# Turning the operands of the last down projection: tokens by channels at the end

## The reference

```python
x = x + rms_norm(groups @ w_out[l], mix_post_norm[l])
h = rms_norm(x, ffn_pre_norm[l])
up = dwconv3(h @ w_up[l], ffn_conv_w[l], ffn_conv_b[l])
gate, val = jnp.split(up, 2, axis=-1)
f = (jax.nn.gelu(gate, approximate=True) * val) @ w_down[l]
x = x + rms_norm(f, ffn_post_norm[l])
```

## Time and profile before

| | |
|---|---|
| median of 3 runs | 1458.9 us |
| profiled execution, its own time | 1459.32 us |
| its span (first to last instruction) | 1457.5 us |
| TensorE matmuls in flight | 1379.8 us, 95% of the span |
| TensorE weight loads | 1029.9 us, 71% |
| VectorE / ScalarE / GpSimd busy | 924.0 / 587.1 / 551.5 us |
| mean granted TensorE clock | 0.989 of full speed |
| the last down projection, first to last matmul start | 1319.05 to 1443.47 us |

### The profile page before, as it was taken

The page is one execution under the profiler, slowest core; times in us unless marked ns, Lnnn a source line. Parts: engine busy times, 40 slices in busy tenths (PEclk is TensorE's granted clock), DMA queues, the critical chain, the costliest instruction groups (busy, mean ns, idle before and its releaser), DMA issues. The chain is left out here.

```text
span 1457.5 us, 15399 instructions
## 1 busy us (share of the span) xinstructions
PE 1379.8 (95%) x5940; PEld 1029.9 (71%) x5940; DVE 924.0 (63%) x992; ACT 587.1 (40%) x864; POOL 551.5 (38%) x287
## 2 busy tenths in 40 slices
PE   7999988988999999999989998988989999999998
PEld 5587654367788888788876785444768888887886
DVE  6776875547778787711186778655478777874113
ACT  5322454534543434432252226444364434343223
POOL 3221332026344444444552215220463434344443
PEclk9999999999999999999999999999999999999999
DMA  7212301012332323233332222100313333323332
GB/s 256 83 29 65 82 13 31 1 57 59 87 101 87 102 87 101 80 101 98 98 131 57 58 54 50 29 15 1 87 58 98 91 99 89 99 85 95 94 93 85
DMA packets 205538, 112.53 MB, mean 77 GB/s; under 512 B 15303, under 2 KB 202425, under 8 KB 204570
## 3 DMA queue, kind: packets, MB, share of 16 engines
q1 hardware_dynamic: 205466, 111.54, 26.3%
HBM read 105.63 MB, written 2.10 MB: 74 GB/s over the span
## 5 line engine op out<-in xcount | busy, mean ns | idle before, releaser
L509 POOL TENSOR_TENSOR wl<-raw,wh 128x1024 fp32r<-128x1024 f32 x176 | 430.2, 2446 | 700.9 <-ACT wh L588 700.9
L588 ACT ACTIVATE wh<-raw 128x1024 fp32r<-128x1024 f32 x176 | 186.5, 1060 | 563.0 <-PE ps L1095 530.4
L1093 PE MATMUL ps<-gh,wh 128*128 128x512 f32 (+1 forms) x864 | 347.5, 402 | 4.8 <-POOL wl L509 4.8
L1095 PE MATMUL ps<-gh,wl 128*128 128x512 f32 (+1 forms) x864 | 342.6, 396 | 0.0
L1094 PE MATMUL ps<-gl,wh 128*128 128x512 f32 (+1 forms) x864 | 342.3, 396 | 0.0
L1093 PEld LDWEIGHTS ps<-gh,wh 128*128 128x128 f32 (+1 forms) x864 | 161.8, 187 | 49.8 <-issue 8.9
L1094 PEld LDWEIGHTS ps<-gl,wh 128*128 128x128 f32 (+1 forms) x864 | 161.8, 187 | 41.9 <-issue 1.9
L1095 PEld LDWEIGHTS ps<-gh,wl 128*128 128x128 f32 (+1 forms) x864 | 161.6, 187 | 40.7
L1533 DVE TENSOR_TENSOR acc<-acc,sq 128x512 f32<-128x512 f32 x24 | 60.6, 2526 | 191.1 <-ACT sq L632 190.8
L1963 DVE SCALAR_TENSOR_TENSOR cv<-pad,pm,cv 128x512 f32<-128x512 f32 x88 | 130.5, 1482 | 78.7 <-ACT cv L952 78.7
L1093 PE MATMUL ps<-fh,wh 128*128 128x512 f32 x308 | 121.7, 395 | 0.6 <-POOL wl L509 0.6
(11 more groups left out here) (274 smaller groups left out, 2211.3 us busy)
## 6 DMA issues: line engine op xcount, KB each, us to landing
raw<-w_up SPq DMA_DIRECT2D x88, 512.0 KB, 3.8
raw<-w_down SPq DMA_DIRECT2D x32, 512.0 KB, 3.8
raw<-w_in SPq DMA_DIRECT2D x30, 512.0 KB, 3.9
raw<-w_out SPq DMA_DIRECT2D x16, 512.0 KB, 4.3
raw<-w_down SPq DMA_DIRECT2D x16, 384.0 KB, 3.3
xio<-x SPq DMA_DIRECT2D x4, 512.0 KB, 4.1
win<-c_win SPq DMA_DIRECT2D x2, 1024.0 KB, 5.6
TF<-c_tf SPq DMA_DIRECT2D x2, 1024.0 KB, 8.9
```

The source lines that it names most:

```text
L509: nc.gpsimd.tensor_tensor(l, raw[:, slot, :], h.bitcast(F32), ALU.subtract).then_inc(S["lo_ready"], 1)
L588: A(xh[:] if third(lay, n) else wh[:, slot, :], raw[:, slot, :], ACT.Copy).then_inc(S["hi_ready"], 1)
L1093: mm(ps[0:cols, bank, :], w_hi, x_hi, start=start and k == 0, stop=False)
L1095: ins = mm(ps[0:cols, bank, :], w_lo, x_hi, start=False, stop=stop and k == tile_n - 1)
```

## The change

In the second layer alone:

- The down projection takes a 128 x 128 block of `fh` or `fl` (128 of its channels by 128 tokens) as stationary operand, and 512 columns of a row block of `w_down` as moving one. All eight PSUM banks hold the sum, bank 2 * tt + dh for token tile tt and half dh of the channels. An item is now one row block of 128 x 1024, so there are 22 instead of 24, the last one (`LAST`) in the third place.
- The order: token tile 0 of blocks 0 and 1, then the rest of these, then blocks 2 to 18 with all eight banks each; then all three last blocks (`TAIL`) bank by bank.
- In the up projection of that layer, after steps 4, 6, ... 18, TensorE transposes four blocks of `xT` into bank 0 or 1, and ScalarE copies the bank to `xres` in the next step.
- The end works on tokens by channels: ScalarE squares a bank with the sum over its columns in the same instruction, and makes the inverse root on one column; VectorE multiplies by the gain (loaded once, on all partitions), then scales and adds to `xres`; SyncE stores each 128 x 512 result. The sum of squares on VectorE, the statistics matmuls, GpSimd's additions, the transposes at the end and their copies go.

The diff, cut to its core:

```diff
-    return n in (2, I_OUT + DC - 1, I_UP + 2, ITEMS - 1)
+    return n in (2, I_OUT + DC - 1, I_UP + 2, ITEMS - 1 if lay < DEPTH - 1 else LAST)
...
+    if lay == DEPTH - 1 and n == LAST:
+        return g - 1
...
+LAST = I_DOWN + FC - 1
+TAIL = 3
...
+        xres = [rope[:, i, :] for i in range(5)] + [w3[:, 0:T], w3[:, T:2 * T], h2[:, 0:T]]
...
+                if lay == DEPTH - 1:
+                    for kk in range(FC):
+                        item(lay, I_DOWN + kk, a["w_down"][lay:lay + 1, kk * P:(kk + 1) * P, :].rearrange("o p (c n) -> o p c n", n=P))
+                    sp.wait_ge(S["f_prod"], DEPTH * FC)
+                    sp.dma_start(cv[:].rearrange("p t n -> p (t n)"), a["ffn_post_norm"][lay, :].partition_broadcast(P)
+                                 ).then_inc(S["g_in"], 16)
+                    continue
...
-            for half in range(2):
-                for c in range(0, DC, 2):
-                    cols, at = slice(c * P, (c + 2) * P), slice(half * TC // 2, (half + 1) * TC // 2)
-                    sp.wait_ge(S["o_copy"], half * DC + c + 2)
-                    sp.dma_start(res[:, at, cols], xout[:, at, cols]).then_inc(S["out_sem"], 16)
+            for tt in range(TC):
+                for dh in range(2):
+                    sp.wait_ge(S["o_done"], 2 * tt + dh + 1)
+                    sp.dma_start(res[:, tt, dh * T:(dh + 1) * T], xres[2 * tt + dh]).then_inc(S["out_sem"], 16)
...
-                for n in range(I_UP + 2, ITEMS + 1 if lay < DEPTH - 1 else ITEMS - 1, 2):
+                for n in range(I_UP + 2, ITEMS + 1 if lay < DEPTH - 1 else LAST, 2):
                     for slot in range(2):
                         lo(lay * ITEMS + n + slot, slot)
-                add(lay, 1)
+                if lay < DEPTH - 1:
+                    add(lay, 1)
...
+                    if lay == DEPTH - 1 and 4 <= j < 20 and j % 2:
+                        g = (j - 4) // 2
+                        act.wait_ge(S["xt_tr"], g + 1)
+                        A(xres[g], ps[:, g % 2, :], ACT.Copy).then_inc(S["xt_copy"], 1)
...
+                if lay == DEPTH - 1:
+                    for n in range(I_DOWN + 3, LAST + 1):
+                        hi(lay, n, n % 2)
+                    continue
...
-            last_square(DEPTH - 1, 1, 0)
-            post(DEPTH - 1, 1, 0)
-            last_square(DEPTH - 1, 1, 1)
-            turned(0, range(2))
-            post(DEPTH - 1, 1, 1)
-            turned(0, range(2, DC))
-            turned(1, range(DC))
+            for tt in range(TC):
+                s0, s1, part, log, r = (st[:, tt, i:i + 1] for i in range(5))
+                act.wait_ge(S["y_done"], 2 * tt + 1)
+                C.do(A(yt[:, 0, :], ps[:, 2 * tt, :], ACT.Square, accum_out=s0))
+                C.join()
+                nc.scalar.sem_inc(S["y_sq"], 1)
+                C.do(A(part, s0, ACT.Identity, bias=eps[:, 0:1], scale=1.0 / DM))
+                act.wait_ge(S["y_done"], 2 * tt + 2)
+                C.do(A(yt[:, 1, :], ps[:, 2 * tt + 1, :], ACT.Square, accum_out=s1))
+                C.join()
+                nc.scalar.sem_inc(S["y_sq"], 1)
+                C.do(A(log, s1, ACT.Ln, bias=part, scale=1.0 / DM))
+                C.join()
+                A(r, log, ACT.Exp, scale=-0.5).then_inc(S["r_inv"], 1)
 
...
+            def turn_stream(g):
+                tt, dh = divmod(g, 2)
+                if g == 0:
+                    pe.wait_ge(S["rbc_ready"], 2 * DEPTH)
+                if g >= 2:
+                    pe.wait_ge(S["xt_copy"], g - 1)
+                for c in range(4):
+                    ins = nc.tensor.transpose(ps[:, g % 2, c * P:(c + 1) * P], xT[:, dh * 4 + c, tt * P:(tt + 1) * P], ident[:])
+                ins.then_inc(S["xt_tr"], 1)
+            def last_down(lay):
+                def part(kk, tt, dh):
+                    h, l = weights(lay, I_DOWN + kk)
+                    bank, rows, cols = 2 * tt + dh, slice(tt * P, (tt + 1) * P), slice(dh * T, (dh + 1) * T)
+                    mm(ps[:, bank, :], fh[:, kk, rows], h[:, cols], start=kk == 0, stop=False)
+                    mm(ps[:, bank, :], fl[:, kk, rows], h[:, cols], start=False, stop=False)
+                    return mm(ps[:, bank, :], fh[:, kk, rows], l[:, cols], start=False, stop=kk == FC - 1)
+                def ready(kk):
+                    item_ready(lay, I_DOWN + kk)
+                    pe.wait_ge(S["f_hi"], lay * FC + kk + 1)
+                    pe.wait_ge(S["f_lo"], lay * FC + kk + 1)
+                pe.wait_ge(S["xt_copy"], DC)
+                for kk in range(2):
+                    ready(kk)
+                    for dh in range(2):
+                        part(kk, 0, dh)
+                pe.wait_ge(S["f_evac"], (lay + 1) * 2 * FC)
+                for kk in range(FC - TAIL):
+                    if kk >= 2:
+                        ready(kk)
+                    for tt in range(1 if kk < 2 else 0, TC):
+                        for dh in range(2):
+                            ins = part(kk, tt, dh)
+                    ins.then_inc(S["pe_item"], 1)
+                for kk in range(FC - TAIL, FC):
+                    ready(kk)
+                for tt in range(TC):
+                    for dh in range(2):
+                        for kk in range(FC - TAIL, FC):
+                            ins = part(kk, tt, dh)
+                        ins.then_inc(S["y_done"], 1)
 
...
+                    if lay == DEPTH - 1 and 4 <= j < 20 and j % 2 == 0:
+                        turn_stream((j - 4) // 2)
...
+                if lay == DEPTH - 1:
+                    last_down(lay)
+                    continue
...
-            for half in range(2):
-                for c in range(DC):
-                    if c % 2:
-                        pe.wait_ge(S["x_new"], 4 * DEPTH * DC + (half * DC + c + 1) // 2)
-                    else:
-                        pe.wait_ge(S["x_own"], (half * DC + c) // 2 + 1)
-                    i = half * DC + c
-                    if i >= 2:
-
-                        pe.wait_ge(S["o_copy"], i - 1)
-                    for t in range(TC // 2):
-                        at = half * T // 2 + t * P
-                        ins = nc.tensor.transpose(ps[:, c % 2, t * P:(t + 1) * P], xT[:, c, at:at + P], ident[:])
-                    ins.then_inc(S["o_tr"], 1)
...
+            dve.wait_ge(S["g_in"], 16)
+            for i in range(TC):
+                for dh in range(2):
+                    dve.wait_ge(S["y_sq"], 2 * i + dh + 1)
+                    if i:
+                        dve.wait_ge(S["o_done"], 2 * i + dh - 1)
+                    tt(ytmp[dh], ps[:, 2 * i + dh, :], cv[:, dh, :], ALU.mult).then_inc(S["y_gain"], 1)
+                dve.wait_ge(S["r_inv"], i + 1)
+                for dh in range(2):
+                    dve.wait_ge(S["y_gain"], 2 * i + dh + 1)
+                    x = xres[2 * i + dh]
+                    stt(out=x, in0=ytmp[dh], scalar=st[:, i, 4:5], in1=x, op0=ALU.mult, op1=ALU.add).then_inc(S["o_done"], 1)
 
 
```

More of the change, by code:

```diff
@@ L90, in freed @@
     return g + 1
+LAST = I_DOWN + FC - 1
+TAIL = 3
+assert LAST % 2 == 1
 HALF = [slice(0, T // 2), slice(T // 2, T)]
@@ L162, in build @@
         nm = sb("nm", [P, 2, TC])
+        st = sb("st", [P, TC, 5])
         with ExitStack() as s:
@@ L251, in build @@
         ysave = probT0
+        xres = [rope[:, i, :] for i in range(5)] + [w3[:, 0:T], w3[:, T:2 * T], h2[:, 0:T]]
+        ytmp = [sq[:, 0, :], sq[:, 1, :]]
         groot = [rbc[:], cv[:, 1, :], rbc[:]]
@@ L268, in build @@
                 "x_new", "gh_ready", "gl_ready", "xsq", "xsq_used", "xstat", "rbc_ready",
-                "y_half", "x_own", "ysq", "ysq_used", "ycopy", "stat_post", "rms_post", "t_ready",
+                "y_half", "ysq", "ysq_used", "ycopy", "stat_post", "rms_post", "t_ready",
                 "evac", "conv1", "conv_done", "nsq", "nstat", "nstd", "nrm", "nperm", "roped", "vtr", "vcopy", "khi", "klo",
@@ L285, in build @@
                 "f_evac", "f_conv1", "f_conv", "f_gelu", "f_prod", "f_hi", "f_lo",
-                "o_tr", "o_copy", "dve_self", "act_self"):
+                "xt_tr", "xt_copy", "g_in", "y_done", "y_sq", "y_gain", "r_inv", "o_done", "dve_self", "act_self"):
             S[name] = sem(name)
@@ L511, in add @@
             def add(lay, b):
-                last = (lay, b) == (DEPTH - 1, 1)
                 for half in range(2):
                     for c in range(DC):
-                        if (c % 2 == 0 if last else c == half == 0):
+                        if c == half == 0:
                             continue
@@ L971, in _ @@
                         n = I_DOWN + 3 * m + i
-                        if (m or i) and (m < DC - 1 or i < 2) and (lay < DEPTH - 1 or n + 2 < ITEMS):
+                        if (m or i) and (m < DC - 1 or i < 2):
                             hi(lay, n + 2, n % 2)
@@ L976, in _ @@
                         ysquare(lay, 1, m)
-                if lay < DEPTH - 1:
```

(21 more changed lines are left out.)

## The result

The changed kernel takes 1467.95 us, the median of four runs (1466.78 to 1468.92), against 1459.09 for the kernel before beside it (1458.44 to 1459.3): ratio 1.0051, 95% interval 1.0028 to 1.0074. It is 8.9 us slower. The sign was forecast, the size was not: 1463.0 was predicted, with a range up to 1466.5. A later comparison on another chip gave 1.0072 (1.0055 to 1.0089). Three disturbed executions (two of e5_both, the profiled one among them, and one of e7_tail1) took 3448 us or more and are left out of the ratios.

The account below looks back on a forecast made before the run. The stage was taken as bound by TensorE's matmul issue. Product -1.8, waits +1.9 and +6.4, clock +1.5 and +0.5, transposes +3.6 and tail -8.1 gave +4.0: 1463.0 us, 8-in-10 range 1459.7 to 1466.5.

Parts of the forecast that it names:

- part 2: Start of the last product: item 0 freed late, so TensorE waits at the fourth row block; 1.9 us lost.
- part 3: Ahead of the last 72 matmuls: TensorE waits for items 20 and 21, as items 20 and 18 share a slot; 6.4 us.
- Step 4: TensorE's clock falls to half after the waits: 1.5 us behind the long one, 0.5 us for the early one.
- Part 5: Up projection: 32 transposes in TensorE's stream at 0.107 us each add 3.6 us; their copies on ScalarE are covered.
- Part 6: Tail from the last matmul's start to the end: 5.9 us against 14.03, a gain of 8.1.
- The last three items are ready: Rival, end of the last product: no long wait because item 20 is converted while item 18 is used; 1455.0 us, 6%.
- The clock holds: Rival, last product: waits come without half clock and the early wait mostly goes; +1.2, 1460.1 us, 18%.
- Transposes cost their duration: Rival, up projection: transposes cost 9.1 us in place of 3.6; 1468.4 us, 4%.
- A cheaper repeated operand: Rival, last product: spacing falls to 0.213 us where neighbouring terms share an fh tile, saving 3.5 us; 1459.4 us, 4%.
- step 1: Last product: 528 matmuls at an unchanged 0.2326 us spacing take 122.6 us, a gain of 1.8.

Follow-up runs that it names:

- e5_both: Changed kernel with block 0 taken whole before block 1 and TAIL = 2; ratio to the kernel before 0.9992.
- e7_tail1: Changed kernel with block 0 taken whole before block 1 and TAIL = 1; ratio to the kernel before 1.0001.
- e1: Changed kernel with block 0 taken whole before block 1 in the last product; ratio to the kernel before 1.0024.
- e4: Changed kernel without the 32 transposes of the stream in the up projection and their 8 copies; ratio to the kernel before 1.0024.
- e9: The changed kernel itself again, on another chip; ratio to the kernel before 1.0072.
- e2: Changed kernel with TAIL = 2 in place of 3; ratio to the kernel before 1.0005.
- e3: Changed kernel with 27 further matmuls by a block of zeros ahead of the wait for the last three items; ratio to the kernel before 1.0047.
- e8: Changed kernel (TAIL = 3) with item 21's low half made by VectorE, not GpSimd; ratio to the kernel before 1.0069.
- e6: Changed kernel with block 0 whole first, TAIL = 2, item 3 converted before the table load, last low half on VectorE; ratio to the kernel before 0.9971.
- e11: Changed kernel, block 0 whole first, TAIL = 2, item 3 converted before the table load, last low half on VectorE, run again; ratio to the kernel before 0.9955.

## Why the prediction was right and wrong

| step | predicted, us | measured, us |
|---|---|---|
| 1 product, 527 spacings | -1.8 | -1.4 (527 x 0.2335 - 124.42) |
| wait for the second block's weights | not seen | +2.44 |
| 2 wait at the fourth block | +1.9 | +1.72 |
| 3 wait ahead of the last 72 | +6.4 | +6.39 |
| 4 clock behind the last wait | +1.5 | +2.6 (2.1 to 2.3 in e1, e4, e9) |
| 4 clock behind an early wait | +0.5 (that of 2) | +1.6 (the one not seen), 0 (that of 2) |
| 5 transposes | +3.6 | +3.4 |
| 6 tail | -8.1 | -8.3 |
| the stages ahead | 0 | +0.3 |
| sum | +4.0 | +8.8 |

The measured column is one profiled execution against one. The +0.3 of the stages ahead is chance: the start of this up projection varies by 5.3 us between kernels that are the same up to there.

**The failed step is part 2.** It says that the first two items "start with token tile 0 of each, so item 0 is free only after 30 matmuls", and follows what item 0's late release does to items 2 and 3. The same reordering does a second thing, which the step never asked: item 1 is wanted after 6 matmuls, 1.4 us, where in the kernel before it was wanted after 18, 4.2 us. Its conversion can't start before the last up item has been used (0.26 us into the product) and takes 3.53 us more, the very terms of part 3: ready at 3.79. 3.79 is under 4.2 and far over 1.4. The missing term, 3.79 + 0.14 - 1.40 = 2.5 us with the hand-over of part 3, was to be had from rows already quoted; it measured 2.44. e1 shows that it is this.

**The clock was undersized.** Step 4 took the fall after the long wait as sure, and it came in all four profiles that have that wait whole and nothing in it (changed, e1, e4, e9). But its price there was 19.21 us for 71 steps that take 16.58, 2.6 in place of 1.5: the half clock lasted 6.8 us, of which 1.1 passed in the wait and 5.7 behind it, where step 4 had taken 3.2. In e1, e4 and e9 it lasted 6.8 us too, with 4.6 to 5.0 of it behind the wait, for 2.1 to 2.3 us. All of that is inside the bounds given (0 to 3). The fall at the early waits was given a third of a chance for a wait of 1.9 us. Behind that wait, 1.72 us as measured, it never came in the six profiles that have it. The one of 2.44 us was what made it: 66 steps and 1.72 of wait would be 17.13 us and took 18.73, 1.6. Of six profiles with that gap (changed, e2, e3, e4, e8, e9), three show a fall behind it and three none, as the two rows of waits of 2.44 and 2.35 us had it. As far as six profiles tell, the odds are even, and the fall is 1.6 of the 1.9 us between the changed kernel's two stretches, 143.6 and 141.7.

**What held.** Part 3, with its mechanism (e2: the wait goes with the third block; e8: part of it with GpSimd's second subtraction). That it came to 0.01 us is luck: xl was ready 6.03 us after N, not 6.26, and TensorE took 0.36 us to go on (1441.00 to 1441.36), not 0.14. Part 5: 0.107 us for each transpose from a distance of starts, and nothing for the copies (e4). By the duration of 272 ns that the trace gives each, it would have been 8.7: that is what the duration gives, not what a transpose takes from a full stream. The Trainium skill's page "TensorE: Matmul & The Clock Gate", section "Part 4: PE-mode transpose", has about 275 ns for a transpose inside a kernel, and this trace agrees with it as a duration. Part 6 to 0.2: the accumulated sum is an instruction of its own of 0.19 us, and the bounds of the forecast had it at 0 to 0.6.

**The rivals.** "The last three items are ready" is excluded by the gap of 6.62. "The clock holds" is excluded by the windows, "Transposes cost their duration" by e4. "A cheaper repeated operand" is excluded by the spacing: 0.2333 throughout, 0.0007 more than before. The kernel's own trace of before gives 0.2333 in the up projection (conversions 5.60 us apart), so the 0.4 us by which step 1 missed were to be had there. The range, 3.5 us above the forecast, held the two known waits. One more with its fall, 2.4 + 1.1 us, used all of it, and the 1.1 us of the last fall and 0.4 of the product came on top.

**What the change is worth.** The turned product and the short tail are a gain: with all waits gone (e6, e11), -9.8 us in the stretch for 3.4 us of transposes. The order of the items, chosen to cover the evacuation of PSUM and the tail, spent 10.6 us in waits and 4.2 in the clock.

## What to carry to other kernels

When a loop is reordered, write down for each loaded item both when it is last used and when it is first wanted; the prediction did the first for item 0 and never the second for item 1. A block held back to shorten the tail has to be paid ahead of it with a wait, as long as conversion after the last release, if no buffer is free: take as few as the engine behind can follow (here 2 blocks, 2.8 us of matmuls for 2.5 of VectorE). And price a wait on TensorE with the half clock behind it: here 2.1 to 2.6 us on top of 6.4.

## What the runs showed of the hardware

- A wait of 2.3 us idle on TensorE was followed by a fall to 1.2 GHz in three of six profiles of the same gap, for 3.4 us each time; a wait of 1.72 us lost in none of six. In the wait of 6.2 us idle the clock fell in four of four, for 6.8 us each time; with the wait cut by 1.2 us (e8) it fell once in one, for 3.4 us.
- Matmuls by a stationary block of zeros in that wait kept the clock at 2.4 GHz (e3, 27 matmuls), and the 72 behind them ran at full speed.
- A wait for a semaphore can stand in the trace as "issue": the gap of 2.29 us did, and went away with the weights' lateness (e1).
- VectorE's subtraction of 128 x 1024, begun beside one of GpSimd, took 1.99 us and ended 1.08 us after GpSimd's (e8); in e6 it took 2.05 and ended 1.08 us after.
- A 128 x 128 transpose lasts 0.272 us, but four of them put into a full stream of matmuls delay it by 0.43 us (changed kernel), and 32 make the up projection 3.4 us longer (e4).
